# A mixed layer kernel whose first-phase products are formed in three passes of high and low parts

## The reference

```
hn = rmsnorm(x, g_mix);  proj = hn @ w_in            # 1024 -> 4000
q_a,k_a,v_a (512 each), c_q 256, c_kv 128, k_pe 32, gate_a, gate_b (1024 each)
y_a = attention(rope(norm q_a), rope(norm k_a), v_a)   # 8 heads of 64
q_b = norm(c_q) @ w_uq;  kv = norm(c_kv) @ w_ukv       # 8 heads of 96 / 64+64
y_b = causal_attention(q_b, k_b, v_b)
merged = sigmoid(gate_a)*(y_a @ w_branch_a) + sigmoid(gate_b)*(y_b @ w_branch_b)
x = x + merged @ w_out
x = x + routed_experts(rmsnorm(x))                     # top 4 of 32, 1024 -> 2 x 1024 -> 1024
x = x + sigmoid(rmsnorm(x) @ w_ple_gate) * (p @ w_ple_proj)
twice: mod = silu(c) @ w_ada + b_ada (shift, scale, gate);  h = rms_norm(x)*(1+scale)+shift
       y = conv/pool mixer(h @ w_in_2) @ w_out_2;  x = x + gate * rms_norm(y)
```

## Time and profile before

| | us |
|---|---|
| median of 3 runs | 1440.49 (1440.48 to 1440.69) |
| the profiled execution, its own time | 1436.58 |
| its span, first to last instruction | 1434.2 |
| PE, DVE, ACT busy in the span | 1360.7, 423.4, 274.7 |
| granted PE clock, mean over the span | 0.99 of full speed |

### The profile page before, as it was taken

One profiled execution on the slowest core, in us unless ns is written; L12 is line 12 of the kernel. 1 busy time (PEld: TensorE's weight loads), 2 busy tenths in 40 slices (PEclk: granted clock), 3 DMA queues, 4 the chain that ended last, 5 costly groups with the idle time before them and its releaser, 6 DMA issues.

```text
span 1434.2 us, 16180 instructions
## 1 busy us (share of the span) xinstructions
PE 1360.7 (95%) x6618; PEld 678.6 (47%) x6618; DVE 423.4 (30%) x661; ACT 274.7 (19%) x392; POOL 30.7 (2%) x50
## 2 busy tenths in 40 slices
PE   8999999999999999999999898999999989999898
PEld 4446644433433343343333333333333336898896
DVE  2344323311211121121112111121112116775774
ACT  2133213110110111111101011010111114532531
POOL 2100010000000000000000000000000000000000
PEclk9999999999999999999999999999999999999999
DMA  9992377899999999999999999999999996355330
GB/s 329 387 341 88 118 265 321 361 416 426 429 428 428 429 429 428 429 428 428 429 428 430 428 430 427 429 429 428 430 428 429 428 413 238 126 179 199 122 124 30
DMA packets 76972, 498.71 MB, mean 348 GB/s; under 512 B 7095, under 2 KB 8586, under 8 KB 52362
## 3 DMA queue, kind: packets, MB, share of 16 engines
q1 hardware_dynamic: 75802, 496.06, 84.6%
q0 software_dynamic: 704, 2.10, 0.4%
q10 hardware_dynamic: 432, 0.07, 0.0%
HBM read 497.06 MB, written 1.05 MB: 347 GB/s over the span
## 4 chain that ended last, share of the span: by engine, by line
PE 69%; DMA 24%; DVE 4%; ACT 2%; issue 1%; POOL 0%; SPq 0%; ACTq 0%; DVEq 0%
PE ps L1621 31%; DMA ring<-in_w_gate_up_dram 24%; PE ps L1386 7%; PE ps L1731 5%; PE ps L1733 5%; PE ps L1732 5%; PE ps L1615 3%; PE ps L1552 2%; PE ps L1536 2%; PE ps L1396 2%; PE ps L1602 1%; PE ps L1686 1%; ACT arena L688 1%; PE ps L1625 1%; PE ps L1365 1%
## 5 line engine op out<-in xcount | busy, mean ns | idle before, releaser
L1621 PE MATMUL ps<-ring,arena 128*64 128x512 f32 x2304 | 515.3, 598 | 28.2 <-DMA ring<-in_w_gate_up_dram 17.1
L1621 PEld LDWEIGHTS ps<-ring,arena 128*64 128x64 f32 x2304 | 159.5, 137 | 356.5 <-issue 304.7
L1621 PE MATMUL ps<-arena 128*64 128x512 f32 x768 | 177.9, 616 | 5.0 <-ACT arena L688 3.1
L1130 DVE TENSOR_SCALAR arena<-ps 128x512 f32<-128x512 f32 x32 | 22.1, 692 | 342.5 <-PE ps L1621 342.5
L681 ACT ACTIVATE arena<-arena 128x512 f32<-128x512 f32 x32 | 20.2, 630 | 491.4 <-DVE arena L1130 491.4
L1386 PE MATMUL ps<-ring,HT 128*128 128x512 f32 (+1 forms) x256 | 111.3, 586 | 1.3 <-ACT HT L594 1.0
L1621 PEld LDWEIGHTS ps<-arena 128*64 128x64 f32 x768 | 54.2, 141 | 119.5 <-issue 105.0
L1733 PE MATMUL ps<-arena_highs,w_low 128*128 128x256 f32 x384 | 108.5, 282 | 0.0
L1091 DVE TENSOR_SCALAR esel<-const 128x128 fp32r<-128x128 f32 x49 | 12.6, 285 | 281.4 <-ACT arena L692 143.5
L692 ACT COPY arena<-ps 64x512 f32<-64x512 f32 x64 | 37.1, 580 | 241.0 <-PE ps L1621 240.6
L1109 DVE TENSOR_TENSOR X<-X,ps 128x1024 f32<-128x1024 f32 x34 | 41.4, 1218 | 121.5 <-PE ps L1615 121.5
(11 more groups left out here) (246 smaller groups left out, 1341.2 us busy)
## 6 DMA issues: line engine op xcount, KB each, us to landing
ring<-in_w_gate_up_dram SPq DMA_DIRECT2D x96, 2048.0 KB, 31.0
ring<-in_w_down_dram SPq DMA_DIRECT2D x48, 2048.0 KB, 33.7
arena<-in_w_gate_up_dram SPq DMA_DIRECT2D x32, 2048.0 KB, 30.7
ring<-in_w_in_dram SPq DMA_DIRECT2D x38, 1024.0 KB, 6.9
arena<-in_w_down_dram SPq DMA_DIRECT2D x16, 2048.0 KB, 34.3
ring<-in_w_ada_dram SPq DMA_DIRECT2D x24, 1024.0 KB, 13.3
ring<-in_w_out_dram SPq DMA_DIRECT2D x12, 1024.0 KB, 6.3
ring<-in_w_ple_gate_dram SPq DMA_DIRECT2D x4, 1024.0 KB, 27.0
```

What stands on the lines that cost most here:

```text
L1621: last = T.matmul(ps[at:at + CAP, bank, :], lhsT, w(g), start=False, stop=stop)
```

## The change

The products of k, lat, v, the gates, the branches and out (22 chunks) are formed in three passes as in the last stage; q, uq and ukv stay plain. The high part of a chunk goes to one of a few places (ring slots 10 and 11, which leave the ring, so that `SLOTS1` is 10, and free parts of the arena and of HN), the low part over the chunk. The table `split1` lists chunk, place, and the chunk that must be used up before the place is free. ACT makes the highs (`w1_high`) at fixed places of its stream, DVE the lows (`w1_low`), in halves within the heads. The columns (hn, y, merged, transposed) are split too. The transposes mT0 stand ahead of the last four-part group of ada1 in front of the out product. SP issues constants and router weights after chunk 3 and w_uq and w_ukv after chunk 7 (before: after 1 and 4). The expert loads start with bins 6 and 4, then 0, 1, 2, 3, and after o1 is used up 5 and 7, and then the 16 small DMAs. Two zeroed tiles move on DVE from ahead of the out product's sum to behind the routing. The diff, cut to its core:

```diff
-SLOTS1 = 12
+SLOTS1 = 10
-        kTb = view(16, HEADS * S, "p (a b) -> p a b", a=HEADS)
+        kTb = view(36, HEADS * S, "p (a b) -> p a b", a=HEADS)
+        colT, yT1, mT1 = [eight(at16), HT_r[:]], [HT_r[:], eight(at8)], [eight(at8), eight(at0)]
+        split1 = [(("k", 0), ring10, None), (("k", 1), ring11, None), (("lat", 0), at0[:], None), (("lat", 1), at8[:], None),
+                  (("v", 0), all_hn, None), (("v", 1), ring10, ("k", 0)),
+                  (("ga0", 0), ring11, ("k", 1)), (("ga0", 1), at8[:], ("lat", 1)), (("ga1", 0), ring10, ("v", 1)),
...
+                  (("A0", 0), at56[:], ("gb0", 1)), (("B0", 0), ring11, ("gb1", 0)), (("A1", 0), ring10, ("gb1", 1)),
+                  (("B1", 0), at64[:], None), (("o0", 0), at56[:], ("A0", 0)), (("o0", 1), ring11, ("B0", 0)),
+                  (("o1", 0), ring10, ("A1", 0)), (("o1", 1), at64[:], ("B1", 0))]
 @@ sync @@
-            for k in range(GROUPS, BINS):
-                load(1, k)
-            for k in range(PER_QUAD):
-                if k < GROUPS:
-                    phase1_left(k)
...
+            load(1, GROUPS)
+            for k in (4, 0, 1, 2, 3):
+                phase1_left(k)
+                load(0, k)
+            sp.wait_ge(s["chunk_used1"], used1("o1"))
+            load(0, GROUPS - 1)
+            load(1, BINS - 1)
+            ada_moved(1)
 @@ scalar @@
+            def w1_high(*c):
+                n, m = at1[c], split_at[c]
+                act.wait_ge(ring1[n % SLOTS1], 16 * (n // SLOTS1 + 1))
+                if split1[m][2]:
+                    act.wait_ge(s["chunk_used1"], at1[split1[m][2]] + 1)
+                A.copy(high1(c), low1(c)).then_inc(s["w1_highs"], 1)
...
+            w1_high("k", 0)
+            w1_high("k", 1)
             act.wait_ge(s["pow_out"], 1)
             normed("q", moba[0])
...
             scaled(filled(act, "latT"), moved1, lambda i: latT[i], 3, lambda i: cols(colA, A_LAT + i))
+            w1_high("ga0", 0)
             act.wait_ge(s["pow_out"], 4)
...
+            w1_high("ga0", 1)
             for h in range(HALVES):
                 p = filled(act, f"kv{h}")
...
+            act.wait_ge(s["y_done"], 2)
+            w1_high("B1", 0)
+            w1_high("o0", 0)
+            w1_high("o0", 1)
+            w1_high("o1", 0)
+            w1_high("o1", 1)
+            column_highs("mT0", mT1[0][:, 0:4, :])
+            column_highs("mT1", mT1[0][:, 4:8, :])
 @@ vector @@
+            def w1_low(*c, part=0, of=1):
+                dve.wait_ge(s["w1_highs"], split_at[c] + 1)
+                n = 4 * chunks1[at1[c]][2] // of
+                here = slice(part * n, part * n + n)
+                V.tensor_tensor(low1(c, ring_low)[:, here], low1(c)[:, here], high1(c)[:, here].bitcast(fp32), ALU.subtract
+                                ).then_inc(s["w1_lows"], 2 // of)
...
+            w1_low("ga0", 1)
+            low_pieces = {(0, 1): [("ga1", 0, 0)], (0, 2): [("ga1", 0, 1)], (0, 4): [("ga1", 1, 0)], (0, 5): [("ga1", 1, 1)],
+                          (0, 7): [("gb0", 0, 0)], (0, 8): [("gb0", 0, 1)],
+                          (8, 9): [("gb0", 1, 0), ("gb0", 1, 1)], (8, 10): [("gb1", 0, 0)], (8, 11): [("gb1", 0, 1)],
...
                     if h < h0 + HEADS:
                         score(h)
+                    for name, kh, part in low_pieces.get((h0, h), ()):
+                        w1_low(name, kh, part=part, of=2)
                     if h > h0:
                         out_of_t(h - 1)
...
+                if g:
+                    w1_low("o0", 1)
+                    w1_low("o1", 0)
+                else:
+                    w1_low("A1", 0)
...
                 dve.wait_ge(s["merged_done"], g + 1)
+                if g == 0:
+                    w1_low("B1", 0)
+                    w1_low("o0", 0)
+            column_lows(2, "mT0", mT1[1][:, 0:4, :], mT1[0][:, 0:4, :])
+            w1_low("o1", 1)
+            column_lows(3, "mT1", mT1[1][:, 4:8, :], mT1[0][:, 4:8, :])
 @@ tensor, project @@
+                    pe.wait_ge(s["w1_lows"], 2 * split_at[(name, kh)] + 2)
+                    high, low = parts1((name, kh))
+                    for h in halves:
+                        for k in range(4):
+                            o, row, at = here(k, h)
+                            T.matmul(o, colT[0][:, row, at], high[:, k, :], start=row == 0, stop=False, skip_group_check=True)
+                            T.matmul(o, colT[0][:, row, at], low[:, k, :], start=False, stop=False, skip_group_check=True)
+                    pe.wait_ge(s["col_lows"], kh + 1)
...
+                            last = T.matmul(o, colT[1][:, row, at], high[:, k, :], start=False, stop=row == KC - 1,
+                                            skip_group_check=True)
```

More of the change, by code:

```diff
@@ L128, in build @@
         pick = rounded("pick", "arena", [P, HALVES, 2, CAP], 22 * 256)
+        ring_low = rounded("ring_low", "ring", [P, SLOTS, SLOT])
+        at0, at8, at16, at56, at64 = [rounded(f"arena_{kb}", "arena", [P, SLOT], kb * 256) for kb in (0, 8, 16, 56, 64)]
         HT_r, HN_r = rounded("HT_r", "HT", [P, KC, S]), rounded("HN_r", "HN", [P, KC, S])
@@ L889, in _ @@
             power()
+            w1_low("ga0", 0)
             moved(dve, "kv0")
@@ L1377, in _, with terms @@
                         last.then_inc(full1[p], 1)
+            def terms(out, lhs, rhs, first, last):
+                T.matmul(out, lhs[0], rhs[0], start=first, stop=False, skip_group_check=True)
+                T.matmul(out, lhs[0], rhs[1], start=False, stop=False, skip_group_check=True)
+                return T.matmul(out, lhs[1], rhs[0], start=False, stop=last, skip_group_check=True)
             def project(gi, kh, halves=(0, 1)):
-                name, n, c = GROUP1[gi], col_groups[gi][1], at1[(GROUP1[gi], kh)]
@@ L1381, in project @@
-                chunk(c)
-                moved(pe, f"hT{kh}")
-                p = free(pe, name)
-                for h in halves:
-                    for k in range(4):
-                        last = T.matmul(ps[:, 2 * p + h, 0:n], HT[:, 4 * kh + k, h * P:h * P + P],
-                                        slot1(c, 4, n)[:, k, :], start=kh + k == 0, stop=4 * kh + k == KC - 1)
+                name, n = GROUP1[gi], col_groups[gi][1]
+                p, c = free(pe, name), at1[(name, kh)]
+                here = lambda k, h: (ps[:, 2 * p + h, 0:n], 4 * kh + k, slice(h * P, h * P + P))
@@ new lines, in project @@
+                if gi == 0:
+                    chunk(c)
+                    moved(pe, f"hT{kh}")
+                    for h in halves:
+                        for k in range(4):
+                            o, row, at = here(k, h)
+                            last = T.matmul(o, HT[:, row, at], slot1(c, 4, n)[:, k, :], start=row == 0, stop=row == KC - 1)
+                else:
+                    pe.wait_ge(s["w1_lows"], 2 * split_at[(name, kh)] + 2)
+                    high, low = parts1((name, kh))
+                    for h in halves:
+                        for k in range(4):
+                            o, row, at = here(k, h)
+                            T.matmul(o, colT[0][:, row, at], high[:, k, :], start=row == 0, stop=False, skip_group_check=True)
+                            T.matmul(o, colT[0][:, row, at], low[:, k, :], start=False, stop=False, skip_group_check=True)
+                    pe.wait_ge(s["col_lows"], kh + 1)
+                    for h in halves:
+                        for k in range(4):
+                            o, row, at = here(k, h)
+                            last = T.matmul(o, colT[1][:, row, at], high[:, k, :], start=False, stop=row == KC - 1,
+                                            skip_group_check=True)
@@ L1527, in _, with columns_of_merged @@
                 features(p, lambda k, h: HN[:, br, h * 512 + k * P:h * 512 + k * P + P]).then_inc(full1[p], 1)
-            for g in range(2):
-                for br, name in enumerate(("A", "B")):
-                    c = at1[(f"{name}{g}", 0)]
-                    chunk(c)
-                    moved(pe, "yTb" if br else "yTa")
-                    p = free(pe, f"{name}{g}")
-                    for h in range(HALVES):
-                        for k in range(4):
-                            last = T.matmul(ps[:, 2 * p + h, :], HT[:, 4 * br + k, h * P:h * P + P],
-                                            slot1(c, 4, 512)[:, k, :], start=k == 0, stop=k == 3)
-                    last.then_inc(s["chunk_used1"], 1)
-                ada_parts(1, 4 * g, 4 * g + 4)
-            for j in range(2):
+            def columns_of_merged(j):
                 pe.wait_ge(s["merged_done"], j + 1)
```

120 lines of the change are left out of this document (92 added, 28 removed), and 1 row of the table low_pieces.

## The result

The changed kernel takes 1424.56 us (median of 4 runs, 1423.35 to 1425.22), the kernel before 1440.49 (4 runs, 1437.58 to 1440.69). The ratio is 0.9898, 95% interval 0.9886 to 0.9910: 1.0% faster. The forecast was 1421 us, range 1412 to 1431. The profiled execution took 1425.22 us, its span is 1423.0. A later repeat of the same kernel gave 1423.79 us and 0.9893 (0.9873 to 0.9913).

A forecast was written before the change was run, and what follows sets the result against it. Matrix products bound the kernel up to the expert stage, weight transfer after it. 30.7 us less matrix work, minus 2.6, 5.1, 0.2, 1.3 and 2, left 19.5: 1436.58 to 1417.1, plus 3.9 gives 1421 us, range 1412 to 1431.

The forecast's parts named there:

- (c): First attention half: DVE is the tight engine; the half ends 7.0 us ahead instead of 12.1, a loss of 5.1.
- The passes: Changed products of the first stage: three passes at 0.696 us a triple give 30.7 us less matrix work.
- (a): Start, k's two chunks: their high and low parts come about when the product needs them; cost 0 to 2 us.
- (b): First scores: kv's moves queue on ACT behind ga0's highs; of 7.9 us won, 5.3 arrive, scores at 80.6.
- (d): Second attention half: DVE and ACT work is hidden behind the product, 5.3 us won, 12.3 ahead.
- (e): Branches to out product: DVE waits for out's first chunk with A1's gate behind; 3.9 us won instead of 5.2.
- (f): Out product: 5.5 us won, first expert at 242.0; the two moved zeroed tiles' 0.4 us lies under fillers.
- (g): Expert weights: bins 5 and 7 asked for last; the stream runs 2 us later against the stage, bounds 0 and 4.
- All hidden: Rival, whole first stage: ACT's and DVE's added work is all hidden, 30.7 - 2, giving 1411.8 us; chance 12%.
- DVE twice as much in the way: Rival, above all first half and out's first chunk: waits double from 9.2 to 18.4 us, giving 1430; chance 20%.
- rival 3: At new gaps in the first stage the clock falls two to four times, costing 3 to 6 us, near 1425; 12%.
- A product in line with its splits: Rival, the 22 split chunks: each could show 4.2 us of DMA, ACT and DVE; at 10 chunks 1454 us; 5%.

The follow-up runs named there:

- experiment 11: The changed kernel itself run again, nothing edited: 1423.79 us, ratio 0.9893.
- experiment 2: The kernel before, products plain, with the 10-slot ring and new order of expert loads, but bins 5 and 7 asked for early: 1438.72 us, ratio 0.9997.
- experiment 3: The changed kernel without DVE's low parts of the 16 chunks of gates, branches and out, still three passes: 1417.16 us, ratio 0.9849.
- experiment 4: The changed kernel with ten small filler matmuls in the matrix engine's gap ahead of ga1's product: 1421.64 us, ratio 0.9881.
- experiments 7: The changed kernel with the out product plain again, its four chunks and merged's columns not split: 1426.79 us, ratio 0.9913.
- experiment 8: The changed kernel with DVE's low parts of the out chunks moved later, the first behind A1's gate: 1422.42 us, ratio 0.9884.
- experiment 9: The changed kernel with the edits of experiment 6 (four fillers at ga1) and experiment 8, ga1's first low parts later, zeroed tiles moved back: 1420.95 us, ratio 0.9877.
- experiment 6: The changed kernel with ga0's second low part earlier, six fillers ahead of the first scores and ten ahead of ga1's product: 1421.08 us, ratio 0.9872.
- experiment 5: The changed kernel with DVE's low part of ga0's second chunk ahead of its wait for kv's moves: 1421.75 us, ratio 0.9882.
- experiment 12: Experiment 9 with low parts of ga1's first chunk back behind scores of heads 1 and 2, and ten fillers at ga1: 1421.20 us, ratio 0.9865.

## Why the prediction was right, and where not

The sign, the range and the main case hold, but not every term does, and two errors in (c) cancelled. By its own steps:

- **The passes.** A triple takes 0.70 us as taken from the earlier trace rows. But the savings of two stretches were priced too high. From the start of k to the end of v it takes 31.5 us instead of 38.8, 7.4 less and not 7.9. A step of the first half is 0.64 us shorter (4.78 against 5.42), so 5.1 us in all, and not 6.8: the prediction compared 3.63 us, in which the last record's own duration is counted, with triples counted from start to start. From its first record to the next instruction's start such a piece takes 3.53 us before and 2.89 after.
- **(a)** DVE starts k's low parts at 20.9 and 23.6 us, as placed. No row shows a wait for them, and none does in experiment 11, where q took 14.00 us and k's product starts at 23.50. In the profiled execution q took 16.34 us instead of 13.97, and the end of v is 4.8 us ahead instead of 7.9 (7.3 in experiment 11). No step had this slow start, and it is not of the change: experiment 2, with plain products, shows the same 16.34.
- **(b)** Right, but the profiled execution doesn't show its mechanism. There the first scores start at 81.31 (predicted 80.6), and PE is idle for 1.30 us, as long as before (1.29): ACT's last move of kv waited 0.43 us for PE. With the fast start of experiment 11 ACT works without a break from 72.83 us on, ga0's two highs and the moves in the order of (b), PE waits 2.71 us, and the first scores start at 80.27.
- **(c)** ga1's product starts at 102.85 (predicted 102.9) behind a gap of 3.1 us (predicted 4). That the two starts agree to 0.1 us owes something to the slow start; in experiment 11 it is 101.80, behind 3.09 us. That DVE's low parts make the gap is shown by experiment 3. The end of the half was 2 us off: 1.6 of it is the clock, shown by experiment 4. The step said that after ga1's product DVE would set the pace; PE did, and at half clock. Two terms were mis-sized against each other: 6.8 us of passes, where the steps show 5.1, and 5.1 us of waits, where 3.0 is shown for DVE's low parts (experiment 3) and some 0.5 more is left without them. Their net of 1.7 us came out, but for the clock, and that is luck.
- **(d)** Right: from the second half's first scores to A0 it took 43.8 us before and 39.2 after, 4.6 less; of the 5.3 expected, 0.7 is lost ahead of A0, at yTa's low part, which (A0) had 0.2 for.
- **(e)** The mechanism is right and is shown by experiments 7 and 8: DVE's queue with A1's gate behind the first out chunk. The term was mis-sized by 1.2 us: the chunk landed 19.9 us after A0 instead of 18.7 (7.5 us for one chunk), and the out product has an effective start of A0 + 34.2 instead of 33.0.
- **(f)** Between the out product's effective start and the first expert 4.3 us are won, not 5.5. 0.4 of the miss are the two zeroed tiles, which stand at 243.1 and 243.6 on DVE's chain. I had called their 0.4 us hidden under the matrix engine's fillers; the row says that PE waits for DVE (0.19 us, L1205) after them, and with the tiles back in their place the 0.4 us is gone (experiment 9). The rest is spread: 0.3 in the out product (17.4 ahead at 228.85, 5.2 more than at its start), 0.3 at a wait of 0.26 us at 231.01, 0.2 up to 233.74. What causes these three was not looked into.
- **(g)** This is the step that failed. I wrote "2 us later, bounds 0 and 4"; the runs show 4.1 in the changed kernel, 5.1 with plain products, and none with bins 5 and 7 early. I had counted when the first refill could land and set the old kernel's dry queue against it as a loss. But the dry queue was the sign that all bins were there. At the first expert the changed kernel had moved 67.9 MB and the kernel before 71.6. That is 3.6 MB, 8.5 us at 428 GB/s. In the next 40 us, in which the old kernel's queue was dry at first, the changed kernel moved 16.8 MB against 14.3, which gives back 5.8 us. 2.7 us are left, and by its last weights' product the changed kernel has moved 0.5 MB more than the old one by its own (454.8 against 454.3), 1.2 us. Together that is the lag, but for 0.2 us.

So of 30.7 us less matrix work the sum left 19.5, and the spans show 11.2. The 8.3 us between are 0.5 ahead of the first scores, 1.6 to the second half (the clock; the two errors in (c) cancel in it), 0.5 ahead of A0 beyond what was counted, 1.2 in (e), 1.2 in (f), 2.1 in (g), 1.2 behind the last weights (0.9 of it in the last expert's product), rounded. By the medians the forecast of 1421 lay 3.6 us low. The 4.7 us between the two accounts are where the profiled executions lay in their runs: 2.4 of them are the faster start of before's, the rest isn't assigned.

**The rivals.** All hidden (1411.8) falls by experiment 3. DVE twice as much in the way (1430) didn't happen. The clock (rival 3) did, once, with 1.6 us in the first half, half of the low end of its 3 to 6 us; the fall in the last expert (0.9 us) comes with plain products too. Its 1425 is nearer to the result than my 1421, but by luck, since most of my miss is (e), (f) and (g). The fall also is one of the signs that I had named for being wrong, a granted clock under 1 before 240 us. A product in line with its splits (1454) didn't happen: within the products the triples run back to back. The Trainium skill (TensorE: Matmul & The Clock Gate, "HAM oscillation") warns that waits between groups of matmuls bring the half clock back. The trace agrees at 102.85 us and, with the fillers, in the other direction.

## What to carry to other kernels

When work is taken from the engine that sets the pace and given to one that looks 30% busy, read that engine's queue in order of time: here it cost 7 us of some 30 (experiment 3), through splits and waits that stood ahead of work that others needed, and through a fall of the clock behind one of these waits. If the next stage ends with its last byte, what counts is how many of its buffers have been asked for when it begins: a queue that is dry at that point is full stock, and a buffer given up for the change costs its share of transfer at the end (4 to 5 us here, more than the split of the out product had won). And a new gap in front of a product costs more than its own length when the clock falls behind it, so order first, and fill what is left, with no more fillers than the gap holds (experiment 6).

## What the runs showed of the hardware

- **The start at half pace.** The first product's 32 records took 13.97 us in some executions and up to 16.34 in others, with plain and with split products (15.57 in experiment 3, 15.69 in experiment 9), while the granted clock reads 1.00. Windows of before and of after from 9 to 12 us:

```profile
9.00:12.00 3.00, 2.76 (x7) 1.35 (x8) 0.79 (x2) 2.17 (x5) 0.00 (x0) 1.00 0.87 266
```

```profile
9.00:12.00 3.00, 2.53 (x3) 1.18 (x4) 1.02 (x2) 3.00 (x6) 0.00 (x0) 1.00 0.87 272
```

Three matmuls started instead of seven. The profiled execution of before was one with the fast start, and with plain products the 2.4 us go through to the first expert (263.5, against 265.97 in experiment 2). In the changed kernel they mostly meet the wait ahead of the first scores: 80.27 against 81.31. The Trainium skill (TensorE: Matmul & The Clock Gate, "What's actually happening") says that the number of slow matmuls at a kernel's start differs from run to run; the trace agrees, though its clock rows don't show it.

- **A gap doesn't decide the fall alone.** Behind 2.70 us idle ahead of the first scores the clock fell in experiment 5 and behind 2.47 us in experiment 8, behind 2.71 us at the same place it stayed up in experiment 11; behind 1.37 us it stayed up in experiment 6 and fell in experiment 12. At a gap of 3.1 us at ga1 it fell all three times (the changed kernel, experiments 7 and 11). At half clock the records are 0.43 us apart, as the Trainium skill has it (same page, "Wait — 56ns, not 53.3ns?": 426.7 ns at 512 columns); at full clock these triples show 0.23.
